# Sums over all partitions in a decoder layer: one fp32 product with ones, or two fp32r products with a high and a low part

## The reference

```
x += 1/2 * rmsnorm(SwiGLU_1(rmsnorm(x)))
p  = rmsnorm(x) @ w_in             # q, k, v, o-gate, conv a and b, gates
mLSTM, 4 heads of 256:  C_t = f_t C_{t-1} + i_t k_t v_t^T,  n_t = f_t n_{t-1} + i_t k_t
        h_t = o_t * (q_t C_t) / max(|n_t . q_t|, exp(-m_t))
conv, 1024 channels:  GLU -> causal depthwise conv (31 taps) -> layernorm over channels -> silu
x += rmsnorm(concat[mLSTM, conv] @ w_out)
x += 1/2 * rmsnorm(SwiGLU_2(rmsnorm(x)))
```

## Time and profile before

| | |
|---|---|
| median of 3 runs | 2153.66 us (2153.62 to 2154.33) |
| the profiled execution | 2154.55 us |
| its span, first to last instruction | 2152.8 us |
| granted clock of TensorE, mean | 1.000 |
| busy PE, DVE, ACT, POOL | 2145.0, 982.1, 891.3, 959.4 us |
| DMA | 377.69 MB, mean 175 GB/s |

### The profile page before, as it was taken

How to read it: one execution, slowest core, us unless ns; L and a number is a source line. 1 busy time by engine, 2 the same in 40 slices (tenths; PEclk the granted TensorE clock), 3 DMA queues, 4 the chain that set the end, 5 groups by cost and what they waited for, 6 DMA issues and landing times.

```text
span 2152.8 us, 41799 instructions
## 1 busy us (share of the span) xinstructions
PE 2145.0 (100%) x16248; PEld 2134.2 (99%) x16248; DVE 982.1 (46%) x1422; ACT 891.3 (41%) x1151; POOL 959.4 (45%) x563
## 2 busy tenths in 40 slices
PE   9999999999999999999999999999999999999998
PEld 9999999999999999999999999999999999999998
DVE  6533432223434324987769738543432223333323
ACT  6434333334343335644345446434333333333443
POOL 1444443434444445476756332444443334444444
PEclk9999999999999999999999999999999999999999
DMA  7454455545554554566766554555455545454653
GB/s 250 165 169 162 164 168 169 163 161 172 164 167 158 174 165 149 204 195 237 242 198 223 200 164 145 170 165 167 157 172 169 166 157 171 161 173 157 210 165 130
DMA packets 121860, 377.69 MB, mean 175 GB/s; under 512 B 28552, under 2 KB 33804, under 8 KB 120496
## 3 DMA queue, kind: packets, MB, share of 16 engines
q1 hardware_dynamic: 97632, 349.00, 49.2%
q10 hardware_dynamic: 24016, 27.42, 4.0%
q0 software_dynamic: 128, 0.07, 0.0%
HBM read 361.26 MB, written 15.18 MB: 175 GB/s over the span
## 4 chain that ended last, share of the span: by engine, by line
PE 99%; DVE 0%; DMA 0%; SPq 0%; ACT 0%; issue 0%
PE bank L484 30%; PE bank L482 30%; PE bank L483 30%; PE bank L537 1%; PE bank L544 1%; PE bank L548 1%; PE bank L826 1%; PE bank L828 1%; PE bank L827 1%; PE bank L748 0%; PE bank L707 0%; DMA raw<-stream 0%; PE bank L689 0%; DVE x_res L1416 0%; DVE bank L1415 0%; PE bank L732 0%
## 5 line engine op out<-in xcount | busy, mean ns | idle before, releaser
L1864 POOL TENSOR_TENSOR wlo<-raw,whi 128x1024 fp32r<-128x1024 f32 x331 | 794.5, 2402 | 851.8 <-ACT whi L898 771.9
L482 PE MATMUL bank<-xh,whi 128*128 128x288 f32 x3344 | 992.2, 297 | 0.0
L483 PE MATMUL bank<-xl,whi 128*128 128x288 f32 x3344 | 988.3, 296 | 0.0
L484 PE MATMUL bank<-xh,wlo 128*128 128x288 f32 x3344 | 986.4, 295 | 0.0
L898 ACT ACTIVATE whi<-raw 128x1024 fp32r<-128x1024 f32 x652 | 687.3, 1056 | 597.6 <-PE bank L484 555.1
L1317 DVE TENSOR_TENSOR wlo<-raw,whi 128x1024 fp32r<-128x1024 f32 x323 | 469.4, 1455 | 769.5 <-ACT whi L898 768.2
L482 PEld LDWEIGHTS bank<-xh,whi 128*128 128x128 f32 x3344 | 630.2, 188 | 2.4 <-issue 2.2
L484 PEld LDWEIGHTS bank<-xh,wlo 128*128 128x128 f32 x3344 | 629.7, 188 | 0.0
L483 PEld LDWEIGHTS bank<-xl,whi 128*128 128x128 f32 x3344 | 628.7, 188 | 0.2
L484 PE MATMUL bank<-hh,wlo 128*128 128x288 f32 x1408 | 417.4, 296 | 0.0
L482 PE MATMUL bank<-hh,whi 128*128 128x288 f32 x1408 | 416.1, 296 | 0.0
(11 more groups left out here) (262 smaller groups left out, 1264.1 us busy)
## 6 DMA issues: line engine op xcount, KB each, us to landing
raw<-stream SPq DMA_DIRECT2D x654, 512.0 KB, 3.6
C<-c_in ACTq DMA_DIRECT2D x4, 2048.0 KB, 8.8
cs_out<-C ACTq DMA_DIRECT2D x4, 2048.0 KB, 8.9
y_out<-x_res SPq DMA_DIRECT2D x7, 288.0 KB, 2.8
bc<-row_copy ACTq DMA_DIRECT2D x4, 448.0 KB, 8.9
conv_out<-upad ACTq DMA_DIRECT2D x4, 302.0 KB, 5.5
upad<-conv_in ACTq DMA_DIRECT2D x4, 272.0 KB, 3.8
vtok<-turned_v ACTq DMA_DIRECT2D x8, 128.0 KB, 3.1
```

The source lines that it names most:

```text
L482: pe.matmul(out, wh, mov_hi[:, k, :], start=first, stop=False)
L483: pe.matmul(out, wh, mov_lo[:, k, :], start=False, stop=False)
L484: return pe.matmul(out, wl, mov_hi[:, k, :], start=False, stop=last)
L1864: pool.tensor_tensor(wlo[:, g % SLOTS, :], raw[:, g % SLOTS, :], whi[:, g % SLOTS, :].bitcast(F32), ALU.subtract).then_inc(lo_ready[g % SL ...
```

## The change

Eight of the nine sums become two fp32r products each, which accumulate in the same bank: ones x high part, then ones x low part (`sums_of`). Only the mixer's norm keeps its fp32 product. `ones` is now an fp32r tile, which the old users read through a view as fp32; POOL makes it with a `tensor_scalar` from the zeroed `ident` instead of a memset. The operands:

- feed-forward norms: after the tree DVE writes high and low part (`two_parts`), and the sum stands two blocks later in PE's queue.
- denominators: ACT copies the high part `den_hi` at k = 13, DVE subtracts for `den_lo` at k = 14, PE waits for `den_low`.
- layer norm: DVE makes both parts of `ysum` and of the squares. PE now waits for `mean_two` where it waited for POOL's `ysum_added`, and DVE waits for POOL and for the stores of the convolution state, whose buffer `ln_two` shares.

`sq` moves into the arena; `den_lo`, `den_hi`, `xsq` and `ln_two` lie in buffers that are unused at the time.

```diff
+            def sums_of(out, high, low):
+                pe.matmul(out, ones_r[:, :], high, start=True, stop=False)
+                return pe.matmul(out, ones_r[:, :], low, start=False, stop=True)
...
-                            if k == (7 if g == 0 else 11):
+                            if k == (9 if g == 0 else 13):
                                 pe.wait_ge(xsq_sum, sums)
-                                feature_sums()
+                                feature_sums(False)
...
             def denominators(h):
-                pe.wait_ge(st_ready, h + 1)
                 pe.wait_ge(sums_ready, h + 1)
-                out = bank[7]
-                pe.matmul(out[:, 0:P], ones[:, :], st[:, 0:P], start=True, stop=False, skip_group_check=True)
-                pe.matmul(out[:, P:TOK], ones[:, :], scr[:, 4, P:TOK], start=False, stop=True, skip_group_check=True)\
-                    .then_inc(num_done, 1)
+                pe.wait_ge(den_low, h + 1)
+                sums_of(bank[7][:, 0:TOK], den_hi[:, :], den_lo[:, :]).then_inc(num_done, 1)
...
             def ln_mean():
-                pe.wait_ge(ysum_added, 2 * H)
-                pe.matmul(bank[4][:, 0:TOK], ones[:, :], ysum[:, :], start=True, stop=True).then_inc(ln_sum, 1)
+                pe.wait_ge(mean_two, 1)
+                sums_of(bank[4][:, 0:TOK], ln_two[:, 0, :], ln_two[:, 1, :]).then_inc(ln_sum, 1)
...
+                if k == 13:
+                    act.wait_ge(sums_ready, h + 1)
+                    act.activation(den_hi[:, 0:P], st[:, 0:P], ACT.Copy)
+                    act.activation(den_hi[:, P:TOK], scr[:, 4, P:TOK], ACT.Copy).then_inc(den_high, 1)
...
+            def two_parts(t, src):
+                link(dve.tensor_copy(t[:, 0, :], src))
+                return dve.tensor_tensor(t[:, 1, :], src, t[:, 0, :].bitcast(F32), ALU.subtract)
...
+                if k == 14:
+                    dve.wait_ge(den_high, h + 1)
+                    dve.tensor_tensor(den_lo[:, 0:P], st[:, 0:P], den_hi[:, 0:P].bitcast(F32), ALU.subtract)
+                    dve.tensor_tensor(den_lo[:, P:TOK], scr[:, 4, P:TOK], den_hi[:, P:TOK].bitcast(F32), ALU.subtract)\
+                       .then_inc(den_low, 1)
...
                 if p == MIX - 7:
+                    dve.wait_ge(ysum_added, 2 * H)
+                    dve.wait_ge(conv_stored, 16 * H)
+                    two_parts(ln_two, ysum[:, :]).then_inc(mean_two, 1)
                     dve.wait_ge(ln_sum, 1)
...
-                    dve.tensor_tensor(lnb[:, 0, :], lnb[:, 0, :], lnb[:, 1, :], ALU.add).then_inc(ln_pair, 1)
+                    link(dve.tensor_tensor(lnb[:, 0, :], lnb[:, 0, :], lnb[:, 1, :], ALU.add))
+                    two_parts(ln_two, lnb[:, 0, :]).then_inc(ln_pair, 1)
```

More of the change, by code:

```diff
@@ L191, in hybrid_layer_kernel @@
         vec = sb("vec", [P, VEC])
-        ones = sb("ones", [P, P])
+        ones_r = sb("ones", [P, P], F32R)
+        ones = ones_r[:, :].bitcast(F32)
         ident = sb("ident", [P, P])
@@ L201, in hybrid_layer_kernel @@
         nfac = sb("nfac", [P, 4])
-        sq = sb("sq", [P, 2, TOK])
         scr = sb("scr", [P, 7, TOK])
@@ L212, in place @@
             return t
+        sq_at = arena[0]
+        sq = place("sq", [P, 2, TOK])
+        den_lo = place("den_lo", [P, TOK], F32R, sq_at + 4 * TOK)
         xl_at = arena[0]
@@ L226, in hybrid_layer_kernel @@
         y_end = arena[0]
+        xsq = place("xsq", [P, 2, TOK], F32R, y_at + 4 * TOK)
         assert arena[0] <= nc.sbuf_usable_end, arena
@@ L249, in hybrid_layer_kernel @@
         qw = place("qw", [P, DC, 2, NS])
+        den_hi = place("den_hi", [P, TOK], F32R)
         assert arena[0] <= y_end, (arena, y_end)
@@ L264, in hybrid_layer_kernel @@
         lnb = place("lnb", [P, 7, TOK], F32, upad_at)
+        ln_two = place("ln_two", [P, 2, TOK], F32R, upad_at + 4 * 5 * TOK)
         assert upad_at + 4 * 7 * TOK <= arena[0]
@@ L339, in hybrid_layer_kernel @@
                                                     sem("cu_evicted"))
+        den_high, den_low = sem("den_high"), sem("den_low")
         sc_done, st_ready, num_done, rden_ready, ro_ready = (sem("sc_done"), sem("st_ready"), sem("num_done"),
@@ L346, in hybrid_layer_kernel @@
                                                        sem("cp_stored"))
+        mean_two, sq_two = sem("mean_two"), sem("sq_two")
         ln_sum, ln_cent, ln_sq, ln_pair, ln_sqsum = (sem("ln_sum"), sem("ln_cent"), sem("ln_sq"), sem("ln_pair"),
@@ L555, in keep_warm, with feature_sums @@
                     pe.matmul(out[:, 0:P], ones[:, :], ones[:, :], start=True, stop=True)
-            def feature_sums():
-                pe.matmul(bank[4][:, 0:TOK], ones[:, :], y[:, 0, :], start=True, stop=True).then_inc(norm_sum, 1)
+            def sums_of(out, high, low):
+                pe.matmul(out, ones_r[:, :], high, start=True, stop=False)
+                return pe.matmul(out, ones_r[:, :], low, start=False, stop=True)
+            def feature_sums(at_mixer):
+                if at_mixer:
+                    pe.matmul(bank[4][:, 0:TOK], ones[:, :], y[:, 0, :], start=True, stop=True).then_inc(norm_sum, 1)
+                else:
+                    sums_of(bank[4][:, 0:TOK], xsq[:, 0, :], xsq[:, 1, :]).then_inc(norm_sum, 1)
             def token_sums(src, first, last, rest=0):
@@ L767, in ln_mean @@
             def ln_mean():
-                pe.wait_ge(ysum_added, 2 * H)
-                pe.matmul(bank[4][:, 0:TOK], ones[:, :], ysum[:, :], start=True, stop=True).then_inc(ln_sum, 1)
+                pe.wait_ge(mean_two, 1)
+                sums_of(bank[4][:, 0:TOK], ln_two[:, 0, :], ln_two[:, 1, :]).then_inc(ln_sum, 1)
             def ln_squares():
                 pe.wait_ge(ln_pair, 1)
-                pe.matmul(bank[4][:, 0:TOK], ones[:, :], lnb[:, 0, :], start=True, stop=True).then_inc(ln_sqsum, 1)
+                sums_of(bank[4][:, 0:TOK], ln_two[:, 0, :], ln_two[:, 1, :]).then_inc(ln_sqsum, 1)
             updates = {(16, 1): 0, (16, 4): 1, (16, 7): 2, (17, 2): 3, (17, 5): 4, (18, 0): 5, (18, 3): 6, (18, 6): 7}
@@ L798, in between @@
                     pe.wait_ge(xsq_sum, 2)
-                    feature_sums()
+                    feature_sums(True)
                     gate_sums()
@@ L1423, in square_tree @@
                     ins = dve.tensor_tensor(y[:, 0:n, :], y[:, 0:n, :], y[:, n:2 * n, :], ALU.add)
-                    if n > 1:
+                    if n > 1 or k != 2 * XC:
                         link(ins)
@@ L1428, in square_tree @@
                     n //= 2
+                if k != 2 * XC:
+                    two_parts(xsq, y[:, 0, :]).then_inc(xsq_sum, 1)
             def evict_scaled(T, tper, i, out, k=None):
@@ L1931, in _ @@
             pool.memset(ident[:, :], 0.0).then_inc(pool_chain, 1)
-            pool.memset(ones[:, :], 1.0).then_inc(ssq_added, SQ_BUFS)
             pool.memset(sel[:, :], 0.0).then_inc(sel_zero, 1)
@@ L1936, in _ @@
             pool.wait_ge(pool_chain, 1)
+            pool.tensor_scalar(ones_r[:, :], ident[:, :], 0.0, 1.0, ALU.mult, ALU.add).then_inc(ssq_added, SQ_BUFS)
+            pool.wait_ge(ssq_added, SQ_BUFS)
             pool.affine_select(out=ident[:, :], in_=ident[:, :], compare_op=ALU.not_equal, fill=1.0, base=0,
```

## The result

The changed kernel takes 2162.91 us (median of 6 runs, 2162.56 to 2164.19), the kernel before on the same chip 2153.72: the ratio is 1.0043, with an interval of 1.0033 to 1.0053. It is 9.2 us slower. The forecast was 2159.6 and the range ended at 2162.8: the direction was right, and the size was not. The profiled execution took 2162.96 us (span 2161.2); the one of before took 2154.55.

What follows compares the result with a forecast made beforehand. TensorE, busy 100% of the span, was taken as the bound; other engines' work is free until it waits. Saved products (-1.84) and waits summed to +5.9 us on 2153.66: 2159.6 us, own range 2158.8 to 2160.6, wider range 2157.3 to 2162.8.

Steps and rivals of the forecast that it cites:

- The products, -1.84: Eight changed sums: each fp32 product of 0.49 us becomes two of 0.13, saving 0.23 each, 1.84 us in all.
- First norm, 0: First feed-forward norm: the sum moves 0.8 us later, as long as its operand pair takes, so nothing waits.
- Head 0, +0.3: Head 0's denominators: operand ready at 936.2, PE there at 935.9; 0.3 us lost, between 0 and 0.6.
- The mean, +2.2: Layer norm's mean: VectorE's subtraction is held up behind GpSimd's weight split; PE stands 2.2 us, between 0 and 2.4.
- a sign of being wrong: Listed as showing the prediction wrong: a CAST taking 0.3 us beside a running split.
- The squares, -0.2: Layer norm's squares: operand ready before the late PE comes, so the earlier 0.2 us wait goes.
- the scores, +0.15: Before head 3's scores: VectorE's last query eviction comes about 0.15 us too late.
- Head 3, +4.9: Head 3's denominators: low part queued behind VectorE's RECIPROCAL and eight multiplications; PE stands 4.9 us, between 4.5 and 5.2.
- the floor: Head 3's stand had nothing else moved: low part ready at 1187.8, PE there at 1183.31, 4.5 us.
- rival B: Array falls to half rate after head 3's stand, costing 1.4 or 2.8 us more: 2161.0 to 2162.4; chance 0.22.
- The last norm, +0.4: Last norm: GpSimd's split of piece 12 starts 0.8 us later, so PE waits 0.4 us, between 0 and 0.5.
- Rival D: Not slower: head 3's low part is ready before PE comes, with the mean on time; 2151.9 to 2153.4; chance 0.12.

Runs made afterwards that it cites:

- experiment 1: Changed kernel, with head 3's high part made earlier on ScalarE and its low part ahead of the RECIPROCAL on VectorE: 2161.85 us.
- experiment 5: Changed kernel, with the layer norm's mean again as one fp32 product: 2161.03 us.
- experiment 7: Changed kernel, with the mean, head 3's denominators and the last norm again as fp32 products: 2154.80 us, ratio 1.0002 to the kernel before.
- experiment 2: Changed kernel, with twenty fp32 products of ones filling TensorE's stand ahead of head 3's wait for the low part: 2161.08 us.
- experiment 3: Changed kernel, with GpSimd's weight split of piece 86 waiting until VectorE has made both parts of the mean: 2162.50 us.
- experiment 4: Changed kernel, with the last norm again as one fp32 product at its old place: 2162.27 us.
- experiment 6: Changed kernel, with head 3's denominators alone again as fp32 products: 2160.11 us.
- experiment 12: Changed kernel with head 3's denominators as fp32 products, and one GpSimd weight split made to wait for VectorE's split: 2156.97 us.
- experiment 8: Kernel before, with only head 3's denominators in two parts (and the new way of making `ones`): 2160.14 us.
- experiment 11: Two parts only in the first norm and heads 1 and 2, the other sums as in the kernel before: 2153.77 us, ratio 0.9999.

## Why the prediction was wrong, by its own steps

*The products, -1.84: right.* The pairs are 0.13 apart.

*First norm, 0: right* as far as the profile shows: no wait there.

*Head 0, +0.3: came at 0.* VectorE's `qwn` operation (927.47) ran 0.35 us ahead of a GpSimd split in the changed kernel and took 0.29 us, and the sums were ready early. In experiments 1, 5 and 7 a `qwn` operation ran beside one and took 2.4, and waits of 0.5 to 1.0 in head 0 followed. In experiments 2, 3, 4, 6 and 12 it or the `qwn` operation ahead of it was held up as well, for 0 to 0.3 of waiting. The term was within its bounds and hangs on which of two operations is first, in experiment 1 by 0.01 us: that it came at 0 is luck.

*The mean, +2.2: the mechanism right, the size 1.8.* The CAST won the first turn and the subtraction paid the split, as the step said. But it ended 0.3 us behind the split, not 0.8 to 1.0. The wait is 1.7, and 0.1 more goes at the restart, where the second product starts 0.24 behind the first. The Trainium skill (SBUF — State Buffer, "Who interferes with whom") says that issue order decides who blocks, and that a DVE instruction with two SBUF inputs contends with a GpSimd instruction that reads SBUF; the trace agrees for the subtraction, 2.51 us against 0.46 in experiment 3. The CAST took its 0.31 beside a split, which the prediction had called a sign of being wrong. But it started 0.05 ahead of the split in all six kernels where the two meet, so no run shows a CAST that comes second.

*The squares, -0.2, and the scores, +0.15.* From head 2's scores to head 3's the time grew by 1.02. Three sums lie in this stretch (head 2's denominators, mean, squares), so the terms give 1.8 - 0.2 - 0.69 = 0.9. The -0.2 came: before, the squares' product started 0.24 behind the product ahead of it and lost another 0.1 at the restart, now it starts 0.13 behind. No wait stands ahead of the scores of head 3, so the +0.15 did not come; the 0.1 left over stays open.

*Head 3, +4.9: the place right, the size 5.3.* The low part was made right behind the eight multiplications, and the RECIPROCAL started 1.0 us earlier than forecast (1182.42 against 1183.4 to 1183.7). But TensorE came at 1183.16, not at 1185.0: 0.6 was gained at the start of this execution, 0.6 by the sums of the first norm and of heads 0 and 1, 0.1 by head 2's (savings that the step had not counted), and 0.4 and 0.15 less were lost at the mean and the scores. Both engines moved together but for 0.8 us, since ScalarE's root, for which the RECIPROCAL waits, ended 0.7 later than before while TensorE came 0.15 earlier. In experiment 8, with no other sum changed, the stand is the floor's 4.4 to 4.6.

*The step that failed is the one that left the half rate out of the sum.* It was rival B, at 0.22, priced at 1.4 to 2.8 from the start's `keep_warm` products. It came, and cost 2.6: the stretch of head 3 grew by 7.73 = 5.3 + 2.6 - 0.23, rounded. Without it the time would have been 2160.3, inside the forecast's own range, in part by luck: head 0, the mean and the scores came out 0.3, 0.4 and 0.15 below their terms, head 3 and the last norm 0.4 and 0.7 above. B's price was good, its chance was not: "the trace has no stand so long between two bursts" was counted against it, when the longest idle stretch that the trace did have, the start, was followed by half rate. (Products stand 0.21 apart there until 4.8 us, 3.1 us in all and not the 2.7 that B used, although the windows of the start give a granted clock of 1.00: there only the distances show it.) The Trainium skill (TensorE: Matmul & The Clock Gate, "Why this matters for your kernels") warns of just this, and the trace agrees: 0.24 us from one product to the next behind the stand of 5.2 us, against 0.13.

*The last norm, +0.4: cost 1.06.* The first wait loses 0.4 (TensorE was due at 1345.45), as forecast; a second wait for a late piece follows at 1368.57, of 0.4 too, which the step did not look for, and each restart costs 0.1 more. The stretch grew by 0.83 with the 0.23 of the sum in it.

*The sum.* -1.84 + 0 + 1.8 - 0.2 + 0 + 5.3 + 2.6 + 1.06 = +8.7, of the measured +9.2. Some 0.1 more is in heads 0 and 1, where the stretch gained 0.35 of 0.46, and 0.1 between the scores of heads 2 and 3; what is left, about 0.3, is less than what the starts of two executions differ by, and stays open.

*Rival D* held that on time denominators bring the kernel to 2151.9 to 2153.4. Head 3 alone does not decide it: with head 3 as before the kernel was still at 2160.1. And with all three stands gone (7) or none made (11) the sums' gain does not show: in 7 the two short waits take it, and in 11 only 0.1 of 0.7 was measured, with no wait to account for the rest.

## What to carry to other kernels

An operation inserted into a busy engine's queue is paid where it stands, not for what it takes: 0.6 us of subtractions cost 6.1 us behind 5.5 us of other work, and 1.4 us, hardly told from no change, eight instructions further up. Price a stand with the half rate behind it; one of 4 us or more cost another 1.4 to 2.7 us here each time, and filling it with idle products, where it can't be removed, gave 1.8 back. Where two engines exclude each other, a shift of a fraction of a microsecond decides who waits, so a stand that is removed may come back elsewhere (experiments 1 and 6): check the whole of TensorE's waits, and put the order down with a semaphore where it matters (12).

## What the runs showed of the hardware that was not expected

- The clock fell during the stand, so all products behind it were slow from the first on (0.24 apart, in the changed kernel for 5.7 us, in experiment 8 for 3.2). Behind the shorter stands of 2.5 and 2.1 us in experiments 1 and 6 it fell only when the array was at work again, in experiment 1 for 3.2 us. Stands of 0.7 to 1.7 us left it at 1.00.
- A CAST of 128x288 from fp32 to fp32r takes 0.31 us, the subtraction behind it 0.46. A 128-column subtraction that takes 0.28 took 1.81 beside a GpSimd split.
